# Who makes the high parts of the projection weights in two attention layers of a four-layer float32 kernel

## The reference, cut to what matters

```python
xn = rmsnorm(h, norm_mix[layer])
proj = xn @ w_in                     # w_in_fox (layer 0) or w_in_dil (layer 1)
q, k, v, (f_logit), qm = split(proj) # three times 768 columns, 12 (layer 0), 256
mix = fox_attention(q, k, v, log_f)                     # layer 0, 12 heads of 64
mix = dilated_attention(rope(q), rope(k), v)            # layer 1
mem_out = memory_attention(qm, mn, w_mem_kv[layer])     # 4 heads, 256 memory tokens
h = h + concat(mix, mem_out) @ w_out[layer]
h = h + conv_ffn(rmsnorm(h, norm_ffn[layer]), ...)
```

## Time and profile before

| what | value |
|---|---|
| median of three runs | 1713.16 us |
| the profiled execution | 1713.56 us |
| its span, first to last instruction | 1711.7 us |
| TensorE busy, weight loads busy | 99%, 80% of the span |
| VectorE, ScalarE, GpSimd busy | 63%, 44%, 54% |
| mean granted TensorE clock | 0.999 of full speed |
| mixer of layer 0, its prelude included | about 557 to 750 us |
| mixer of layer 1, its prelude included | about 1143 to 1326 us |

### The profile page before, as it was taken

The page is one execution under the profiler, slowest core; times in us unless marked ns, Lnnn a source line. Parts: engine busy times, 40 slices in busy tenths (PEclk is TensorE's granted clock), DMA queues, the critical chain, the costliest instruction groups (busy, mean ns, idle before and its releaser), DMA issues.

```text
span 1711.7 us, 25096 instructions
## 1 busy us (share of the span) xinstructions
PE 1697.3 (99%) x9544; PEld 1377.1 (80%) x9548; DVE 1081.2 (63%) x2171; ACT 754.0 (44%) x1601; POOL 917.4 (54%) x839
## 2 busy tenths in 40 slices
PE   9999999999999999999999999999999999999998
PEld 7886788787689977779888888888777888888886
DVE  6897734795652356434766756866875358477478
ACT  4626523213433244425444444446664345345445
POOL 8525457553347733345654655657344563574474
PEclk9999999999999999999999999999999999999999
DMA  6321323221222321113243144142111323413511
GB/s 187 112 81 45 116 63 106 73 94 55 81 99 88 123 74 50 50 55 95 72 123 124 50 123 123 50 148 91 58 50 50 93 87 105 136 62 101 146 68 55
DMA packets 174983, 152.45 MB, mean 89 GB/s; under 512 B 6104, under 2 KB 149848, under 8 KB 174864
## 3 DMA queue, kind: packets, MB, share of 16 engines
q1 hardware_dynamic: 173264, 149.37, 28.2%
q10 hardware_dynamic: 1600, 1.48, 0.3%
HBM read 147.65 MB, written 2.14 MB: 88 GB/s over the span
## 4 chain that ended last, share of the span: by engine, by line
PE 89%; DVE 5%; ACT 2%; POOL 2%; DMA 1%; issue 1%; SPq 0%; DVEq 0%; ACTq 0%
PE ps L487 73%; PE ps L2465 2%; PE ps L2500 2%; PE ps L2485 2%; POOL w_lo L205 1%; DVE ffn_cv L2941 1%; PE ps L1932 1%; PE ps L558 1%; PE ps L1910 1%; PE ps L2473 1%; PE ps L1847 1%; DMA w_chain<-w_down 1%; PE ps L1034 1%; PE ps L1868 1%; PE ps L1922 0%
## 5 line engine op out<-in xcount | busy, mean ns | idle before, releaser
L487 PE MATMUL ps<-x_hi,w_hi 128*128 128x512 f32 (+2 forms) x1432 | 532.4, 372 | 0.8 <-DVE x_lo L802 0.4
L487 PE MATMUL ps<-x_hi,w_lo 128*128 128x512 f32 (+2 forms) x1432 | 522.5, 365 | 0.0
L487 PE MATMUL ps<-x_lo,w_hi 128*128 128x512 f32 (+2 forms) x1432 | 522.0, 365 | 0.0
L233 POOL TENSOR_SCALAR w_hi<-w_raw 128x512 fp32r<-128x512 f32 x272 | 169.2, 650 | 498.6 <-PE ps L487 477.7
L237 POOL TENSOR_TENSOR w_lo<-w_raw,w_hi 128x512 fp32r<-128x512 f32 x272 | 361.2, 1360 | 5.9
L487 PEld LDWEIGHTS ps<-x_hi,w_hi 128*128 128x128 f32 (+1 forms) x1432 | 269.3, 188 | 60.6 <-issue 16.0
L487 PEld LDWEIGHTS ps<-x_hi,w_lo 128*128 128x128 f32 (+1 forms) x1432 | 269.3, 188 | 44.2
L487 PEld LDWEIGHTS ps<-x_lo,w_hi 128*128 128x128 f32 (+1 forms) x1432 | 269.6, 188 | 40.4
L205 POOL TENSOR_TENSOR w_lo<-w_raw,w_hi 128x512 fp32r<-128x512 f32 x158 | 212.8, 1382 | 139.3 <-ACT w_hi L189 135.6
L2941 DVE SCALAR_TENSOR_TENSOR ffn_cv<-ps,col,ffn_cv 128x510 f32<-128x510 f32 (+1 forms) x176 | 131.7, 749 | 151.7 <-ACT ffn_cv L2885 147.0
L487 PE MATMUL ps<-w_hi,ffn_a_hi 128*128 128x512 f32 x308 | 121.2, 394 | 1.2 <-DVE ffn_a_lo L2962 1.0
(11 more groups left out here) (408 smaller groups left out, 3005.4 us busy)
## 6 DMA issues: line engine op xcount, KB each, us to landing
w_raw<-w_up SPq DMA_DIRECT2D x80, 512.0 KB, 5.1
w_raw<-od_w_in SPq DMA_DIRECT2D x12, 1024.0 KB, 5.1
w_raw<-w_in_fox SPq DMA_DIRECT2D x10, 1024.0 KB, 5.3
w_raw<-w_in_dil SPq DMA_DIRECT2D x10, 1024.0 KB, 5.0
w_raw<-w_out SPq DMA_DIRECT2D x8, 1024.0 KB, 4.9
w_raw<-w_down SPq DMA_DIRECT2D x8, 1024.0 KB, 5.0
w_raw<-ev_w_in SPq DMA_DIRECT2D x6, 1024.0 KB, 5.4
w_third<-w_down SPq DMA_DIRECT2D x18, 256.0 KB, 5.2
```

The lines of the kernel that those rows point to most:

```text
L233: ins = pool.tensor_scalar(hi[:, c:min(c + PIECE, size)], raw[:, c:min(c + PIECE, size)], 1.0, 1.0, ALU.mult, ALU.mult)
L487: mm = pe.matmul(o, l, r, start=start and i == 0, stop=stop and i == 2, skip_group_check=again)
```

## The change

The slots qm, q1, k1, v1, q2, k2 and v2 of both layers, 14 in all, are added with `hi_by_act`. GpSimd makes only their low parts. ScalarE makes the high part of slot n in its `evacuate`, right behind the evacuation of the last block of slot n-3. The slots q0, k0, the forget gate and v0 stay as they were, and so do those of `w_out`.

```diff
-        def wide(w, c0, width, kd=KD):
+        def wide(w, c0, width, kd=KD, hi_by_act=False):
...
-                W.add(kd, n, [(0, tiles(w, 0, kd)[:, :, c:c + n])])
+                W.add(kd, n, [(0, tiles(w, 0, kd)[:, :, c:c + n])], hi_by_act)
...
-            w_qm[layer] = wide(w_in, 3 * FW + (FH if layer == 0 else 0), 256)
+            w_qm[layer] = wide(w_in, 3 * FW + (FH if layer == 0 else 0), 256, hi_by_act=True)
             for i in range(1, 3):
-                w_q[layer][i] = wide(w_in, 256 * i, 256)
-                w_k[layer][i] = wide(w_in, FW + 256 * i, 256)
-                w_v[layer][i] = wide(w_in, 2 * FW + 256 * i, 256)
+                w_q[layer][i] = wide(w_in, 256 * i, 256, hi_by_act=True)
+                w_k[layer][i] = wide(w_in, FW + 256 * i, 256, hi_by_act=True)
+                w_v[layer][i] = wide(w_in, 2 * FW + 256 * i, 256, hi_by_act=True)
...
                         act.activation(dst, ps[:, bank, 0:dst.shape[1]], ACT.Copy).then_inc(self.evacuated.s, 1)
+                    if self.ends[m] and w_qm[self.layer] <= slot + SPLIT <= w_v[self.layer][2]:
+                        W.high(act, slot + SPLIT)
```

## The result

The changed kernel takes 1717.16 us, the median of 13 runs (1716.87 to 1717.71). The kernel before, run beside it, takes 1713.28 us (13 runs, 1713.08 to 1714.17). The ratio is 1.0022 with a 95% interval of 1.0014 to 1.0029: 3.9 us or 0.22% slower. The profiled execution of the changed kernel took 1716.93 us, its span is 1715.1 us, and the granted clock is 0.999 as before.

What follows compares the result with a forecast made beforehand. TensorE was taken to bound the kernel, never waiting for GpSimd in a mixer. Waits of 1.4 + 1.6 + 0.5 = 3.5 us gave 1716.7 us, with 1713.3 to 1718.5 as the range for 8 in 10.

Steps and rivals of the forecast that it cites:

- What bounds the kernel: Whole kernel: TensorE, busy 99%, waits for GpSimd nowhere in a mixer, so GpSimd's work is off the path.
- What is removed: 28 of GpSimd's 48 high pieces leave each mixer; nothing waited for them, gain 0, at most 0.4 us.
- Groups that fit: Most steps of both layers: copies 2.1 us later still end before TensorE's transposes, 1.4 to 1.6 us to spare, cost 0.
- Step 6: Layer 1: copies behind the high pieces come late, so the next transposes wait 1.4 us.
- Step 10: Layer 1: late copies delay the next transposes by 1.6 us, range 0.5 to 1.9, as most ScalarE work moves along.
- Prelude: Layer 1: exponential 2.3 us later and longer scalings make TensorE's scores wait 0.5 us, bounds 0 and 1.4.
- the sign: Near 1179 in layer 1: one TensorE wait of up to 1.4 us, released by VectorE's logits.
- The sum: Whole kernel: 1.4 + 1.6 + 0.5 = 3.5 us of new TensorE waits, bounds 1.8 to 4.8 us.
- Absorbed: Layer 1, transposes of steps 7 and 11: ScalarE's delay never reaches TensorE, 1713.2 us; chance 0.17.
- Relieved: VectorE is relieved of GpSimd, only layer 0's 0.4 us wait goes, 1712.8 us; chance 0.03.
- Room too small elsewhere: Six groups that fit by 1.4 to 1.6 us each cost 0.5 us more, 1719.7 us; chance 0.11.
- the edge of the 3.4 us: Whole kernel: a measurement can tell 0.2%, 3.4 us, from no change; the forecast lies just over.

Runs made afterwards that it cites:

- l0_only: Changed kernel, but only layer 0's seven slots get high parts from ScalarE, layer 1 as before the change; 1713.11 us beside 1713.32 for the kernel before.
- twice_l0: Changed kernel, but every high piece of v1, q2, k2 and v2 of layer 0 is made twice; 1722.09 us beside 1713.39 for the kernel before.
- two_and_two: Changed kernel, but in the steps two high pieces stand ahead of the transposes' copy and two behind; 1716.28 us beside 1713.69 for the kernel before.
- twice_l1: Changed kernel, but every high piece of q2 and k2 of layer 1 is made twice; 1725.82 us beside 1713.39 for the kernel before.
- half_more_l1: Changed kernel, but two of four high pieces of q2 and k2 of layer 1 are made twice; 1722.29 us beside 1713.69 for the kernel before.

## Why the prediction was right

**What bounds the kernel.** Right. TensorE never waited for GpSimd in a mixer, and taking 38 us of work from GpSimd gave 0.4 us at most.

**What is removed: 0.** Off by 0.4 us, which the text had as the most it could be. The stretch is 0.42 us shorter, by 0.2 us of the wait for the logits and by transposes of step 0 that no longer stretch while they wait for the second scaling (0.38 us against 0.62). GpSimd's low pieces now end before that scaling. l0_only repeats it. The 0 overlooked that the low pieces do not only become ready earlier or later for TensorE: their times move against VectorE's instructions, to the good here and to the bad in layer 1.

**Groups that fit: 0.** Right. No wait for ScalarE in layer 0 and none in layer 1's steps 2 and 14. The room was smaller than the 1.6 us named for step 6 of layer 0: twice_l0 puts it at 1.2. The start at 633.48 was read from the chain, which lets a piece begin where the one ahead ends; the timeline has those transposes begin at 633.32 and their weight loads at 633.09.

**Step 6: 1.4 us.** 1.37 measured, and right in its mechanism too.

**Step 10: 1.6 us**, chosen between 0.5 and 1.9: 1.61 measured between the weight loads, with an idle time of 1.28 us in it. The number is right, the reason is not. The forecast let ScalarE's row move along because TensorE came later. The row did move, by 1.04 us from the evacuation of step 6 to that of step 10 (19.90 us in place of 18.86). But VectorE's rotation in step 6 alone is 1.03 us longer (1.72 and 1.65 us against 0.69 and 1.66). And in two_and_two, where TensorE's transposes of step 7 came 0.4 us later and not 1.4, the row moved by the same 1.03. So it was VectorE beside GpSimd's low pieces that pushed ScalarE, which no term of the sum had. That the choice between 0.5 and 1.9 came out right was luck.

**Prelude: 0.5 us**, between 0 and 1.4: 1.22 measured, and this is the term that was mis-sized. Two steps of it failed. The exponential came 2.75 us later, counted from the scores of step 0 (4.57 us behind them in place of 1.82), and not 2.3: the idle time ahead of v0's last evacuation did not take up all the delay of the two earlier groups, so that this evacuation ended 0.55 us later before the third group began. And the two scalings took 0.59 us more together, not 0.4, since the low pieces did not end in the middle: they lay beside both. 2.75 + 0.59 = 3.34, less the 2.15 us that VectorE's logits had to spare before (ready at 1176.6, wanted at 1178.8), makes 1.2. On TensorE it shows as 0.6 us for the scaling and 0.4 us for the logits, where one wait for the logits was named as the sign. The rule quoted there from the Trainium skill, SBUF — State Buffer, section "SBUF: two separate sides", put the term at its lower bound; the trace is against that use of it, since what stands beside the scalings now are GpSimd's low pieces, and the rule makes no difference between high and low pieces. It does agree where it says that ScalarE never waits for the port: the groups of four took 2.18 to 2.20 us wherever they stood.

**The sum.** 1.4 + 1.6 + 0.5 = 3.5 was forecast, 1.37 + 1.61 + 1.22 - 0.42 = 3.8 by the trace, 3.9 by the medians. The two misses, 0.7 us too little in the prelude and 0.4 us of gain left out, went against each other. The bounds printed as 1.8 and 4.8 are 1.9 and 4.7 by the terms given (1.4 + 0.5 + 0 and 1.4 + 1.9 + 1.4), which changes nothing.

**The rivals.** Absorbed: refuted by the two waits, 1.25 and 1.28 us. Relieved and nothing else: refuted by the same waits. Room too small elsewhere: refuted for the change, and made real by twice_l0. That the forecast lay on the edge of the 3.4 us is borne out: 3.9 us were measured.

## What to carry to other kernels

A busy share does not say what work an engine can take. Read instead, for each place where the work would stand, when the next instruction behind it ends and when the engine that waits for that one gets there; the difference is the room, and it held here to 0.4 us at the places in the steps that were tested (in the prelude, where VectorE stands between, it was off by 0.7). Take the moment of arrival from the timeline and not from the chain. Put the work behind the instruction that others wait for and look at once which one is next: behind the copies it cost 1.5 us in place of 3.9, but not nothing. Look as well at when the relieved engine's remaining work now runs, and beside what: here it shortened one scaling and made a rotation 1.03 us longer. And where the bounding engine never waited for the engine that is relieved, there is little to win: 0.4 us here.

## What the runs showed of the hardware

- TensorE's clock fell from 2.4 to 1.2 GHz when work came back after waits of 3.89 us (twice, twice_l1) and after one of 2.58 us, but not after another wait of the same length in the same kernel (half_more_l1), nor after any of 1.3 us. Each fall cost 1.7 us. So a wait on the bounding engine cost 1.4 to 1.7 times its length here where the clock fell, and whether a 2.6 us wait does so cannot be told from its length alone.
- Beside GpSimd's low pieces VectorE's instructions took longer or not by where they began: a multiplication of 128x512 with two operands in SBUF took 1.72 us when a low piece had begun 0.11 us ahead of it (1210.53 and 1210.64, change), and 0.69 us in the kernel before, where the low pieces had run since 1209.10. A scaling of 128x128 took 0.29 us with no low piece beside it (597.69, change) and between 0.59 and 1.28 us with one, in the cases shown.
- A wait of TensorE behind matmuls of 512 columns cost 0.16 us more than its printed idle time (records of 0.39 us, starts 0.23 us apart), and the eight transposes behind it took 1.07 us in place of 1.03.
